# Expert stage: the third weight remainder of a block's first step goes behind the accumulation of the block before

## Chip, cores and metric

The kernel runs on one core of a Trainium2 chip. The metric is the device time of one execution in microseconds. The core has five engines with a queue of instructions each: TensorE (matmuls), VectorE, ScalarE, GpSimd and SyncE (here it only issues transfers). They are ordered against each other by semaphores. A queue is worked off in its order: an instruction that waits holds back those behind it.

## What is computed

The reference is two networks in a row on 512 tokens of 1024 features. The change lies in the last part of the first one, a mixture of 16 experts in 4 groups of 4. Each token goes to one group and in it to two experts:

```python
hid = jax.nn.silu(jnp.einsum('td,edf->tef', t, w_gate)) * jnp.einsum('td,edf->tef', t, w_up)
hid = hid * combine[..., None].astype(hid.dtype)
y = jnp.einsum('tef,efd->td', hid, w_down)
```

An expert has 256 hidden features, so its gate and up weights are 1024 x 512 together and its down weights 256 x 1024.

## The kernel before

**Blocks and steps.** Tokens are sorted by their group and cut into four blocks of 128 rows. Since a group's tokens may straddle blocks, seven passes (`STAIRS`; called blocks here, number i) cover all pairs of a row block and a group that can occur, and each pass has four steps, one for each expert of its group. So there are 28 steps, x = 0 to 27, and i = x // 4. Which row block and which group a pass has is read from tables at run time.

**Slabs.** A step needs three slabs of weights of 128 x 2048 numbers (1 MB): two for gate and up (`gate_slab(x, 0)`, `gate_slab(x, 1)`), one for down (`down_slab(x)`). They are numbered q in the order of use. Matmuls are done in three products, on a rounded part and a remainder of each operand. So each slab passes through four hands:

- SyncE loads it into one of six buffers (line 2054). The load of slab q waits until the remainder of slab q - 6 is done (`moe_lo`).
- ScalarE writes the rounded part into one of four buffers (`moe_split`, line 2543), once the slab that had the buffer, q - 4, has been used (`moe_used`).
- VectorE subtracts and writes the remainder (`moe_rest`, line 2924), which counts up `moe_lo`.
- TensorE waits for `moe_lo` and uses both.

**A step on TensorE** (loop at line 2308): the first half of gate and up of x (12 matmuls of 512 columns, lines 2266 to 2268), the transposition of the hidden values of x - 1 (line 2278), the second half of gate and up of x (12), and the down product of x - 1 (`down`, lines 2293 to 2295, 12 matmuls). The down products of a block's four steps add up in two PSUM banks. The one of the next block's first step, e == 0, overwrites them, and waits before that for `moe_acc`:

```python
                if e == 0 and i:
                    pe.wait_ge(moe_acc, i)
                pe.wait_ge(moe_hT_lo, x + 1)
```

**A step on VectorE** (loop at line 2973), in the order of its queue: the remainder of the transposed hidden values of x - 1 (`hidT_lo`, line 2976; it waits for ScalarE's rounded copy, line 2564); where x % 4 == 1 and i > 0, the accumulation of block i - 1 (`add_pair`, lines 2963 to 2971): it reads an address from a table into a register (line 2967) and adds the two banks to the sum in SBUF, then raises `moe_acc`; the remainder of the slab four behind the step's first one; the product of the gate, the up half and the routing weight (line 2997), which waits for ScalarE's Silu (line 2585) and is what TensorE transposes; and two more remainders, of the slab four behind the step's second one and four behind `down_slab(x - 1)`.

So at x = 4, whose numbers are used below, the three remainders are of the slabs 15, 16 and 17, and at x = 5 of 18, 19 and 20. Slab 17 is the first gate and up slab of x = 6, 18 the second, 19 the down slab of x = 5, 20 the first slab of x = 7.

The order on each engine is written out by hand; nothing is placed by a planner. GpSimd has no instruction inside the loop.

Of the kernel before, what the change touches and what calls it, by code (L numbers as in the profile page):

```python
# [42 lines left out]
GROUPS, PER_GROUP = 4, 4  # L43
STAIRS = TB + GROUPS - 1
EXPERT_STEPS = STAIRS * PER_GROUP
MOE_SLABS = 3 * EXPERT_STEPS
MOE_RAW, MOE_W = 6, 4
# [49 lines left out]
def gate_slab(x, part):  # L97

    return x * 3 - 1 + part if x else part


def down_slab(x):

    return 3 * x + 4 if x < EXPERT_STEPS - 1 else MOE_SLABS - 1
# [44 lines left out]
def build(nc, t):  # L149
    with ExitStack() as whole:  # L150
# [53 lines left out]
        def v1(name, i=0, rows=slice(0, P)):  # L204
            return vec[rows, V1[name].start + i:V1[name].start + i + 1]
# [2624 lines left out]
        def _(dve):  # L2830
# [91 lines left out]
            def moe_rest(q):  # L2922
                dve.wait_ge(moe_hi, q + 1)
                dve.tensor_tensor(moe_w_lo[q % MOE_W], moe_raw[q % MOE_RAW], moe_w_hi[q % MOE_W].bitcast(F32),
                                  ALU.subtract).then_inc(moe_lo, 1)
# [37 lines left out]
            def add_pair(i):  # L2963
                dve.wait_ge(moe_used, down_slab(PER_GROUP * i + PER_GROUP - 1) + 1)
                if i:
                    dve.wait_ge(moe_acc, i)
                at = dve.value_load(acc_at[0:1, i:i + 1], min_val=0, max_val=D * (TB - 1))
                for n in range(2):
                    to = acc[:, bass.ds(at + n * TOK, TOK)]
                    ins = dve.tensor_tensor(to, pd[2 + n][:], to, ALU.add)  # L2970
                ins.then_inc(moe_acc, 1)

            for x in range(EXPERT_STEPS + 1):
                if x:
                    dve.wait_ge(moe_hT_hi, x)
                    dve.tensor_tensor(hidT_lo[(x - 1) % 2], px[(x - 1) % 2][:, 0:256],
                                      hidT_hi[(x - 1) % 2].bitcast(F32), ALU.subtract).then_inc(moe_hT_lo, 1)
                if x == EXPERT_STEPS:
                    break
                i = x // PER_GROUP  # L2980
                if x % PER_GROUP == 1 and i:
                    add_pair(i - 1)
                if 1 <= x < EXPERT_STEPS - 1:
                    moe_rest(gate_slab(x, 0) + MOE_W)
                elif x == 0:
                    moe_rest(MOE_W)
                if x == EXPERT_STEPS - 1:
                    for b in range(TB - 1):
                        dve.wait_ge(y_blk_hi, b + 1)
                        dve.tensor_tensor(acc_lo[:, b * D:(b + 1) * D], acc[:, b * D:(b + 1) * D],  # L2990
                                          acc_hi[:, b * D:(b + 1) * D].bitcast(F32), ALU.subtract).then_inc(y_blk_lo, 1)
                if x % PER_GROUP == 0:
                    if i:
                        w_at = dve.value_load(weight_at[0:1, i:i + 1], min_val=0, max_val=W_COLS * TB - 5)
                w = weight[:, x:x + 1] if i == 0 else weight[:, bass.ds(w_at + x % PER_GROUP, 1)]
                dve.wait_ge(moe_silu, x + 1)
                dve.scalar_tensor_tensor(gated[x % 2], gated[x % 2], w, pd[x % 2][:, 256:512], ALU.mult,
                                         ALU.mult).then_inc(moe_hid, 1)
                if x < EXPERT_STEPS - 1:
                    moe_rest(gate_slab(x, 1) + MOE_W)  # L3000
                else:
                    for b in range(TB):
                        ins = dve.tensor_scalar(back[:, b], pos_row, v1("slot", b), None, ALU.is_equal)
                    ins.then_inc(back_ready, 1)
                if 1 <= x < EXPERT_STEPS - 1:
                    moe_rest(down_slab(x - 1) + MOE_W)
            add_pair(STAIRS - 1)
            dve.wait_ge(y_blk_hi, TB)
# [426 lines left out]
```

## Time and profile before

| what | value |
|---|---|
| median of 3 runs | 2624.4 us |
| the runs | 2622.12, 2624.4, 2628.64 us |
| profiled execution | 2626.12 us, its span 2624.3 us |
| TensorE busy | 2577.8 us, 98% of the span |
| VectorE busy | 1546.3 us, 59% |
| ScalarE busy | 1088.5 us, 41% |
| GpSimd busy | 875.4 us, 33% |

The profile is one execution. Its rows name an engine (PE is TensorE's matmuls, PEld its weight loads, DVE VectorE, ACT ScalarE, POOL GpSimd, SP SyncE; a q behind the name is the engine's sequencer), a line of the kernel, the operation and its output and inputs. Times are us from the start of the span. A matmul's row is longer than the distance to the next one, since they are pipelined; the distance of starts is what one costs. The same is so on VectorE and ScalarE, by some 0.1 us.

The expert loop lies between about 420 and 660 us of the span.

### The profile page before, as it was taken

Reading aid. Unit: us, or ns where it says so; the run is one execution under the profiler, and the core shown is the slowest. Engines: PE = TensorE matmul, PEld = TensorE weight load, DVE = VectorE, ACT = ScalarE, POOL = GpSimd, SP = SyncE. Lnnn points to the kernel's source line nnn. Section 1 sums busy time; section 2 is a strip of 40 time slices with the busy share of each in tenths; the row PEclk is TensorE's granted clock in tenths of the full one; section 3 lists DMA queues with packets and bytes.
Section 4 is the critical chain, followed back from the end, with each engine's and each line's share of the span. In section 5 each row is a group of like instructions: output and inputs, shape, how many; then the busy total and the mean of one; then the engine's idle time right before and its main releaser. Section 6 shows DMA issues by size and latency. Waiting matters only on the chain.

```text
span 2624.3 us, 32509 instructions
## 1 busy us (share of the span) xinstructions
PE 2577.8 (98%) x12950; PEld 2124.6 (81%) x12950; DVE 1546.3 (59%) x1716; ACT 1088.5 (41%) x1299; POOL 875.4 (33%) x203
## 2 busy tenths in 40 slices
PE   7999999999999999999999999999999999999998
PEld 5777788888788888888888888888888888888887
DVE  5584637999765483364765437854654464835445
ACT  6333627887425532334432223435433343422222
POOL 0211020000242443445344443433443454344444
PEclk9999988999999999999999999999999999999999
DMA  4240036998221662232333333322652232333332
GB/s 155 105 154 2 1 129 263 368 362 327 77 96 55 222 253 81 96 116 101 113 121 121 120 120 112 109 81 100 245 196 87 96 120 96 113 128 121 120 120 105
DMA packets 61292, 361.13 MB, mean 138 GB/s; under 512 B 7280, under 2 KB 8176, under 8 KB 26096
## 3 DMA queue, kind: packets, MB, share of 16 engines
q1 hardware_dynamic: 58720, 353.49, 37.6%
q10 hardware_dynamic: 2448, 5.90, 0.7%
q8 instruction: 88, 1.44, 0.2%
q14 instruction: 36, 0.29, 0.0%
HBM read 357.25 MB, written 2.10 MB: 137 GB/s over the span
## 4 chain that ended last, share of the span: by engine, by line
PE 81%; DVE 3%; ACT 1%; issue 1%; POOL 1%; DMA 0%; ACTq 0%; DVEq 0%; SPq 0%; POOLq 0%
PE pd L278 20%; PE pd L280 19%; PE pd L279 19%; PE pd L304 2%; PE pd L303 2%; PE pd L302 2%; PE pd L2268 2%; PE pd L2267 2%; PE pd L2266 2%; DVE sb_y_lo L1967 1%; PE pd L2293 1%; PE pd L2295 1%; PE pd L2294 1%; PE pd L2223 1%; PE px L2424 1%
## 5 line engine op out<-in xcount | busy, mean ns | idle before, releaser
L228 POOL TENSOR_TENSOR sb_w_lo<-sb_raw,sb_w_hi 128x2048 fp32r<-128x2048 f32 x175 | 819.3, 4682 | 1596.8 <-ACT sb_w_hi L219 1596.8
L278 PE MATMUL pd<-sb_h_hi,sb_w_hi 128*128 128x512 f32 x1600 | 631.7, 395 | 3.0 <-DVE sb_h_lo L580 2.4
L279 PE MATMUL pd<-sb_h_lo,sb_w_hi 128*128 128x512 f32 x1600 | 624.0, 390 | 0.0
L280 PE MATMUL pd<-sb_h_hi,sb_w_lo 128*128 128x512 f32 x1600 | 623.9, 390 | 0.0
L219 ACT CAST sb_w_hi<-sb_raw 128x2048 fp32r<-128x2048 f32 x181 | 346.1, 1913 | 410.1 <-PE pd L280 311.2
L278 PE MATMUL pd<-sb_y_hi,sb_w_hi 128*128 128x512 f32 x944 | 369.1, 391 | 1.2 <-DVE sb_y_lo L1967 0.8
L280 PE MATMUL pd<-sb_y_hi,sb_w_lo 128*128 128x512 f32 x944 | 367.4, 389 | 0.0
L279 PE MATMUL pd<-sb_y_lo,sb_w_hi 128*128 128x512 f32 x944 | 367.4, 389 | 0.0
L278 PEld LDWEIGHTS pd<-sb_h_hi,sb_w_hi 128*128 128x128 f32 x1600 | 301.0, 188 | 68.6 <-issue 5.2
L280 PEld LDWEIGHTS pd<-sb_h_hi,sb_w_lo 128*128 128x128 f32 x1600 | 301.0, 188 | 63.2
L279 PEld LDWEIGHTS pd<-sb_h_lo,sb_w_hi 128*128 128x128 f32 x1600 | 301.2, 188 | 61.4 <-issue 0.5
L278 PEld LDWEIGHTS pd<-sb_y_hi,sb_w_hi 128*128 128x128 f32 x944 | 177.2, 188 | 41.5 <-DVE sb_y_lo L1967 4.6
L1967 DVE TENSOR_TENSOR sb_y_lo<-sb_T,sb_y_hi 128x512 fp32r<-128x512 f32 x80 | 187.9, 2388 | 35.8 <-ACT sb_y_hi L1941 28.5
L280 PEld LDWEIGHTS pd<-sb_y_hi,sb_w_lo 128*128 128x128 f32 x944 | 177.2, 188 | 37.1
L279 PEld LDWEIGHTS pd<-sb_y_lo,sb_w_hi 128*128 128x128 f32 x944 | 177.2, 188 | 36.4
L2009 DVE SCALAR_TENSOR_TENSOR sb_xT<-pd,sb_lay,sb_xT 128x512 f32<-128x512 f32 x80 | 56.8, 747 | 155.8 <-PE pd L280 152.1
L1936 ACT ACTIVATE sb_T<-pd 128x512 f32<-128x512 f32 x60 | 32.6, 595 | 203.9 <-PE pd L280 203.9
L594 DVE CUSTOM_DVE_ANT_0 sb_QK<-sb_QK,sb_Y 128x1024 f32<-128x1024 f32 x32 | 77.2, 2448 | 67.8 <-ACT sb_Y L2710 44.9
L302 PE MATMUL pd<-sb_w_hi,sb_h_hi 128*128 128x512 f32 x288 | 112.6, 391 | 0.0
L304 PE MATMUL pd<-sb_w_lo,sb_h_hi 128*128 128x512 f32 x288 | 112.1, 389 | 0.0
L303 PE MATMUL pd<-sb_w_hi,sb_h_lo 128*128 128x512 f32 x288 | 112.1, 389 | 0.0
L3241 DVE TENSOR_TENSOR sb_T<-sb_T 128x512 f32<-128x512 f32 x64 | 45.0, 744 | 105.6 <-ACT sb_T L1936 103.6
(591 smaller groups left out, 3740.1 us busy)
## 6 DMA issues: line engine op xcount, KB each, us to landing
sb_raw<-in_slabs SPq DMA_DIRECT2D x190, 1024.0 KB, 4.8
sb_moe_raw<-in_moe SPq DMA_DIRECT2D x56, 1024.0 KB, 6.6
sb_raw<-in_moe SPq DMA_DIRECT2D x28, 1024.0 KB, 6.2
sb_QK<-in_ada SPq DMA_DIRECT2D x32, 512.0 KB, 5.4
sb_V<-in_ada SPq DMA_DIRECT2D x32, 512.0 KB, 5.5
sb_M<-in_ada SPq DMA_DIRECT2D x16, 512.0 KB, 3.9
sb_Y<-in_ada SPq DMA_DIRECT2D x16, 512.0 KB, 5.8
sb_MG<-in_ada SPq DMA_DIRECT2D x16, 512.0 KB, 5.9
```

The costliest lines, as they stand in the source:

```text
L219: act.copy(w_hi[j][:], raw[j][:]).then_inc(w_hi_ready[j], 1)
L228: pool.tensor_tensor(w_lo[j][:], raw[j][:], w_hi[j][:].bitcast(F32), ALU.subtract).then_inc(w_lo_ready[j], 1)
L278: pe.matmul(out, w_hi[j][:, cols], hi[:, k], start=(k == 0), stop=False)
L279: pe.matmul(out, w_hi[j][:, cols], lo[:, k], start=False, stop=False)
L280: last = pe.matmul(out, w_lo[j][:, cols], hi[:, k], start=False, stop=(k == KT - 1))
L302: pe.matmul(pd[b][:], hi[:, k, toks], w_hi[j][:, cols], start=(k == 0), stop=False)
L303: pe.matmul(pd[b][:], lo[:, k, toks], w_hi[j][:, cols], start=False, stop=False)
L304: last = pe.matmul(pd[b][:], hi[:, k, toks], w_lo[j][:, cols], start=False, stop=(k == KT - 1))
L594: dve.tensor_tensor_reduce(tiles[slot], tiles[slot], row, 1.0, 0.0, ALU.mult, ALU.add, into).then_inc(ada_used, 1)
L1967: dve.tensor_tensor(y_lo[:, bass.ds(2 * n + f, 1)], T[:, tj + f:tj + f + 1], y_hi[:, bass.ds(2 * n + f, 1)].bitcast(F32), ALU.subtract).th ...
L2009: ins = dve.scalar_tensor_tensor(to, bank, lay[:, bass.ds(gate + tile + 2 * j + f, 1)], to, ALU.mult, ALU.add)
L2266: pe.matmul(pd[x % 2][:], hi[:, k], moe_w_hi[s][:, cols], start=(k == 0), stop=False)
```

## The change

On VectorE, the remainder of slab `down_slab(x - 1) + 4` is no longer computed at the end of a step with x % 4 == 0, the first step of a block. It is computed in the step behind it, directly behind the accumulation (`add_pair`) of the block before and ahead of that step's first remainder. The slab is the one four behind the down slab of the last step of the block before. This happens in the steps 4, 8, 12, 16, 20 and 24; at x = 0 there is no such remainder. The order of the remainders among themselves stays (15, 16, 17, 18, ...), and so do all counts on the semaphores.

```diff
@@ -2980,6 +2980,7 @@
                 i = x // PER_GROUP
                 if x % PER_GROUP == 1 and i:
                     add_pair(i - 1)
+                    moe_rest(down_slab(x - 2) + MOE_W)
                 if 1 <= x < EXPERT_STEPS - 1:
                     moe_rest(gate_slab(x, 0) + MOE_W)
                 elif x == 0:
@@ -3002,7 +3003,7 @@
                     for b in range(TB):
                         ins = dve.tensor_scalar(back[:, b], pos_row, v1("slot", b), None, ALU.is_equal)
                     ins.then_inc(back_ready, 1)
-                if 1 <= x < EXPERT_STEPS - 1:
+                if 1 <= x < EXPERT_STEPS - 1 and x % PER_GROUP:
                     moe_rest(down_slab(x - 1) + MOE_W)
             add_pair(STAIRS - 1)
             dve.wait_ge(y_blk_hi, TB)
```

## Rows read from the trace of the kernel before

**Rows 1.** The page, busy time of each engine, share of the span, instructions.
```profile
PE 2577.8 (98%) x12950; PEld 2124.6 (81%) x12950; DVE 1546.3 (59%) x1716; ACT 1088.5 (41%) x1299; POOL 875.4 (33%) x203
```

**Rows 2.** Table of stretches (busy us, count; clock, DMA share, GB/s), x = 5 and 6.
```profile
core 0: us, PE busy (x) PEld busy (x) DVE busy (x) ACT busy (x) POOL busy (x), PEclk, DMA share, GB/s
461.30:470.30 9.00, 8.73 (x40) 6.86 (x39) 8.98 (x8) 6.38 (x5) 0.00 (x0) 1.00 0.98 366
470.30:478.70 8.40, 8.40 (x39) 6.93 (x38) 7.36 (x6) 7.33 (x6) 0.00 (x0) 1.00 0.96 363
```

**Rows 3.** Waits in the expert stage: total us, times, longest; TensorE and its weight loads.
```profile
PEld pd L2293 <- issue: 4.0, 6, 0.7
...
PE pd L2293 <- issue: 1.6, 6, 0.3
```

**Rows 4.** Timeline of TensorE: start, duration, instruction [idle before]; first and sixth gap.
```profile
466.80 0.39 PE L2268 MATMUL pd<-sb_moe_w_lo,sb_sorted_blk 128*128 128x512 f32 x1
467.45 0.47 PE L2293 MATMUL pd<-sb_w_hi,sb_hidT_hi 128*128 128x512 f32 x1 [0.27 <-issue]
...
470.30 0.39 PE L2266 MATMUL pd<-sb_w_hi,sb_sorted_blk 128*128 128x512 f32 x1
...
638.51 0.47 PE L2293 MATMUL pd<-sb_w_hi,sb_hidT_hi 128*128 128x512 f32 x1 [0.28 <-issue]
```

**Rows 5.** Timeline of VectorE from the end of x = 4 to x = 7.
```profile
463.53 2.29 DVE L2924 TENSOR_TENSOR sb_w_lo<-sb_moe_raw,sb_w_hi 128x2048 fp32r<-128x2048 f32 x1
465.74 0.41 DVE L2976 TENSOR_TENSOR sb_hidT_lo<-px,sb_hidT_hi 128x256 fp32r<-128x256 f32 x1
466.08 1.28 DVE L2970 TENSOR_TENSOR sb_MG<-pd,sb_MG 128x512 f32 x2
467.27 2.28 DVE L2924 TENSOR_TENSOR sb_moe_w_lo<-sb_raw,sb_moe_w_hi 128x2048 fp32r<-128x2048 f32 x1
469.47 0.47 DVE L2997 SCALAR_TENSOR_TENSOR sb_T<-sb_T,sb_lay,pd 128x256 f32<-128x256 f32 x1
469.86 2.28 DVE L2924 TENSOR_TENSOR sb_moe_w_lo<-sb_raw,sb_moe_w_hi 128x2048 fp32r<-128x2048 f32 x1
472.50 2.29 DVE L2924 TENSOR_TENSOR sb_w_lo<-sb_moe_raw,sb_w_hi 128x2048 fp32r<-128x2048 f32 x1 [0.35 <-ACT sb_w_hi L2543]
474.71 0.42 DVE L2976 TENSOR_TENSOR sb_hidT_lo<-px,sb_hidT_hi 128x256 fp32r<-128x256 f32 x1
...
483.12 0.42 DVE L2976 TENSOR_TENSOR sb_hidT_lo<-px,sb_hidT_hi 128x256 fp32r<-128x256 f32 x1
```

**Rows 6.** Timeline of ScalarE: copy of hidden values, x = 5, and cast of slab 20.
```profile
464.48 0.37 ACT L2564 CAST sb_hidT_hi<-px 128x256 fp32r<-128x256 f32 x1 [0.98 <-PE px L2278]
...
470.55 1.92 ACT L2543 CAST sb_w_hi<-sb_moe_raw 128x2048 fp32r<-128x2048 f32 x1 [1.05 <-PE pd L2295]
```

**Rows 7.** Line 2967, register load, first and last of seven; line 2970, the adds.
```profile
L2967 DVEq TENSOR_LOAD <-sb_small x7: 303/311/327, 464.9 to 665.9; - x7
...
L2970 DVE TENSOR_TENSOR sb_MG<-pd,sb_MG x14: 678/680/692, 466.1 to 667.2; 128x512 f32 x14
```

**Rows 8.** Timeline at the stage's end: last matmul of the last down product, accumulation.
```profile
665.42 0.39 PE L2295 MATMUL pd<-sb_moe_w_lo,sb_hidT_hi 128*128 128x512 f32 x1
...
666.58 1.29 DVE L2970 TENSOR_TENSOR sb_MG<-pd,sb_MG 128x512 f32 x2 [6.28 <-PE pd L2295]
```

**Rows 9.** Timeline of TensorE, x = 6: transposition, down product of step 5, next step.
```profile
473.02 0.38 PE L2278 MATMUL px<-sb_ident,sb_T 128*128 128x128 f32 x2
...
475.99 0.39 PE L2293 MATMUL pd<-sb_moe_w_hi,sb_hidT_hi 128*128 128x512 f32 x1
...
478.71 0.39 PE L2266 MATMUL pd<-sb_w_hi,sb_sorted_blk 128*128 128x512 f32 x1
```

**Rows 10.** Load of slab 23, time to landing (455 to 490 us), cast of slab 23.
```profile
466.01 0.34 SPq L2054 DMA_DIRECT2D sb_moe_raw<-in_moe  x1
...
DMA to landing us min/median/max: 4.8/5.2/6.3
...
478.96 1.92 ACT L2543 CAST sb_moe_w_hi<-sb_moe_raw 128x2048 fp32r<-128x2048 f32 x1 [0.50 <-PE pd L2295]
```

## Prediction

> **What bounds the kernel now.** I read the page first: TensorE is busy for 98% of the span [rows 1], so nothing the change does on VectorE counts unless it opens or closes a gap on TensorE. The stretch that the change touches is the expert stage, where seven blocks of four steps follow each other. The table by step of the second block [rows 2] shows one step of about 8.4 us, and the step in which the accumulation falls is 9.0 us long, with VectorE busy for 8.98 of them against 7.36 in the next. So VectorE is full there and nearly full elsewhere. The list of waits [rows 3] has six gaps of TensorE before the down product (line 2293), 1.6 us together on the matmuls and 4.0 us on their weight loads. They are put down to "issue", but the wait that stands there in the code is the one for `moe_acc`, and the accumulation is what ends just before: the second of its two adds ends at 467.36 and the matmul starts at 467.45 [rows 4, 5]. That is 0.09 us from release to start, which I use below for VectorE to TensorE.
>
> The gap's whole price is read from TensorE's own rows [rows 4]. The last gate/up matmul starts at 466.80. One pitch is 0.227 us (12 matmuls in 2.72 us, 475.99 to 478.71 [rows 9]), so the down product could start at 467.03. It starts at 467.45 and takes until 470.30, 2.85 us instead of 2.72, because the matmuls come a little slower after a stop. The price is 470.30 minus (467.03 + 2.72) = **0.55 us a block**. The same gap stands before the down product of each of six blocks; the last is at 638.51 [rows 4]. All there is to win is 6 x 0.55 = 3.3 us.
>
> **What the change removes and adds.** No instruction is added or dropped. In each block but the first, one 2.21 us remainder (slab 17 in the block that I follow; start to start on VectorE, 463.53 to 465.74 [rows 5]) moves from before `hidT_lo` and the two adds to behind them. SP's ring counts remainders, so one load per block is issued later, too. I write the new order of VectorE out from these rows, in the trace's own times, with x = 5 as the step of the accumulation.
>
> 1. Behind slab 16's remainder VectorE is free at 463.53 at the latest. It now goes straight to `hidT_lo` of step 4, which needs ScalarE's copy: 464.48 + 0.37 = 464.85 [rows 6]. It starts at about 464.88 instead of 465.74, 0.86 us earlier. VectorE stands still for 1.35 us meanwhile, and this is the cost that nothing gives back.
>
> 2. The adds need a register load (line 2967), which the trace shows at 464.9, right after that copy, though VectorE is still in a remainder [rows 5, 7]. It was hidden; now it is partly bare. The case where the load is bare stands at the end of the stage: load 665.9, first add 666.58 [rows 7, 8], 0.68 us. So the first add starts at 464.9 + 0.7 = 465.60, where `hidT_lo` alone would let it start at 464.88 + 0.34 = 465.22 (0.34 from [rows 5]). Bounds: hidden after all, 465.22; begun only when `hidT_lo` is through (465.30), and then the 0.77 us from the last matmul's end, 665.42 + 0.39, to 666.58 [rows 8], 466.07. I take 465.60, because the load was at 464.9 while the engine was busy, so it does not wait for the engine.
>
> 3. The adds end at 465.60 + 1.28 = 466.88 instead of 467.36 [rows 5]. With 0.09 us that is 466.97, before 467.03. **TensorE's gap closes**: down(4) runs from 467.03 to 469.75, and TensorE is 0.55 us ahead.
>
> 4. Then come four remainders and one product until `hidT_lo` of step 5, where there were three and one. By the pitches of [rows 5] (adds 1.19, remainder 2.21, product 0.39): slab 17 at 466.79, slab 18 at 469.00, product at 471.21, slab 19 at 471.60, slab 20 at 473.81, `hidT_lo` of step 5 at **476.02** instead of 474.71. Of the 0.35 us for which VectorE waited for ScalarE before slab 20, nothing is left.
>
> 5. TensorE's needs, shifted by 0.55 us [rows 9]: slab 17 at 469.75 (ready 469.08), slab 18 at 472.61 (471.29), the product for the transpose at 472.47 (471.68), slab 19 at 475.44 (473.89). All met; the tightest has 0.67 us. ScalarE's cast of slab 20 began at 470.55, behind down(4); half a microsecond earlier now, it is no bound [rows 6]. But down(5) also needs `hidT_lo` of step 5, and could start at 475.99 - 0.55 = 475.44. It gets it at 476.02 + 0.42 + 0.09 = **476.53**. This is a new gap of 1.09 us, one step behind the old one.
>
> 6. After that stop down(5) takes 2.85 us again, as down(4) did [rows 4], and ends at 479.38; before it ended at 478.71 [rows 9]. **Net +0.67 us a block.** TensorE's gain in step 5 doesn't enter: the new start hangs on VectorE's chain, which is anchored at the copy of 464.85.
>
> 7. Is it carried on? VectorE goes on at 476.36: slab 21, product, slab 22 until 481.17. Slab 23's cast began at 478.96, 0.25 us behind the end of down(5) [rows 9, 10], so now at 479.63 and until 481.55; the remainder runs to 483.78, and `hidT_lo` of step 6 is there at 484.20 (before 483.12 + 0.42 [rows 5]). Down(6) needs it at 479.38 + 2.72 + 2.97 = 485.07 [rows 9]. From there VectorE waits for ScalarE again, as before. The lateness ends within two steps, and each block pays once.
>
> 8. SP: the load behind slab 17's remainder went out at 466.01; now at about 469.2. Landing took at most 6.3 us [rows 10], so it is there by 475.5, and ScalarE wants it at 478.96. The next ones are 1.2 to 2 us later and have more room. Cost nothing; GpSimd has no work in this stage [rows 2].
>
> Sum: 6 x 0.67 = **+4.0 us**. The profiled execution took 2626.12 us (span 2624.30); it would take 2630.1. The median of the runs, 2624.4, is 1.7 us below the profiled one, and I carry the difference: **2628.4 us**. With the bounds of step 2 the new start moves by -0.38 or +0.47 us: +0.29 a block (1.7 us, 2626.1) to +1.14 a block (6.8 us, 2631.2).
>
> On the register load a page of the Trainium skill can be weighed against the rows: "DMA: Bandwidth & Descriptors", section "Latency and other measured facts", gives a floor of about 600 ns for a `tensor_load`. The trace shows 0.68 us from the load's start to the add at the place where nothing hides it [rows 7, 8]. An estimate by the page would put the adds 0.08 us earlier and the sum at 3.5 instead of 4.0 us.
>
> **Rivals.**
> *The gap goes and nothing replaces it.* This is faster: 6 x 0.55 = 3.3 us, 2621.1 us. It holds if VectorE's chain from 464.88 is 1.1 us shorter than by my pitches. For it: VectorE is busy for only 7.36 us of the step behind [rows 2], so it seems to have a microsecond to spare. Against: that microsecond lies behind step 5's four remainders, and even with the load wholly hidden the chain ends 0.7 us too late. 10 in 100.
> *The load waits for the engine, or a second place is hit.* The upper bound of step 2, +6.8 us, 2631.2 us; slower still only if the slab margin of 0.67 us in step 5 goes as well. At 466.07 for the adds slab 17 would be ready at 469.55, still before 469.75. To reach 0.3% each block would have to lose 1.3 us. 10 in 100.
> *It does nothing.* If VectorE's copy dependence were late enough that the order didn't matter, both gaps would stay as they are, 2624.4 us. The adds' start is set by the remainder in front of them (463.53 + 2.21 = 465.74 [rows 5]), not by the copy at 464.85, so this is unlikely: 5 in 100.
> *The forecast*, a new gap before the down product one step later: 75 in 100.
>
> **How the numbers follow.** About 0.3%, 7.9 us, is what a measurement of this kernel can tell from no change. Neither the whole gain (3.3 us) nor the upper bound (6.8 us) reaches it, so within 0.3% gets 0.94; slower by more needs something beyond the bound, 0.04; faster by more 0.02. The range takes in the bounds 2626.1 and 2631.2, and the scatter of the runs shown (2622.12 to 2628.64 around 2624.4, so 2 to 4 us) on both sides, and most of the gap-only case: 2621.5 to 2633.
>
> **What would show it.** Right: in the trace after, the six gaps before line 2293 sit one down product later; `hidT_lo` starts about 0.9 us sooner in the accumulation's step and 1.3 us later in the next; four remainders stand without a break between the adds and it; a block takes 34.9 us instead of 34.2 (first and sixth gap at 467.45 and 638.51 [rows 4], 171.06 / 5 = 34.21). Step 2 is wrong if the first add does not start 0.7 us behind the copy. The prediction fails if the down product of step 5 starts without a gap (then 2621), or if TensorE also waits for slab 17 or 18 (then above 2631).

## The result, and the profile after

| | before | changed |
|---|---|---|
| median of 20 runs each | 2625.63 us | 2631.20 us |
| ratio | | 1.0023, 95% interval 1.0016 to 1.0030 |
| span of the profiled execution | 2624.3 us | 2629.5 us |
| first to last transposition of the expert stage (line 2278) | 228.2 us | 232.8 us |

The changed kernel is slower by 4 to 8 us (0.23% of 2626 is 6.0 us; the medians are 5.6 us apart). The forecast was 2628.4 us, 4.0 us more than before, and the measured median is 2631.2.

The last row of the table is the measure that I use for all kernels below. It comes from the rows that give the first and the last start of one line, rounded to 0.1 us, so a length can be off by 0.1 us. Before and after:

```profile
L2278 PE MATMUL px<-sb_ident,sb_T x56: 270/271/328, 430.4 to 658.6; 128*128 128x128 f32 x56
```
```profile
L2278 PE MATMUL px<-sb_ident,sb_T x56: 270/271/327, 430.2 to 663.0; 128*128 128x128 f32 x56
```

So 4.6 us are lost between the first and the last of these. The waits of the changed kernel in the stage (total, times, longest) show where, and answer to [rows 3]:

```profile
DVE sb_hidT_lo L2976 <- ACT sb_hidT_hi L2564: 8.3, 6, 1.4
PEld pd L2293 <- DVE sb_w_lo L2924: 7.7, 6, 1.3
...
PE pd L2293 <- DVE sb_hidT_lo L2976: 5.3, 6, 0.9
DVE sb_MG L2970 <- issue: 2.2, 6, 0.4
PEld pd L2293 <- issue: 1.6, 6, 0.3
```

TensorE's idle time before the down product was 1.6 us in six gaps and is 5.3 us in six gaps, and it is now put down to `hidT_lo`. Two waits of VectorE are new: 6 x 1.4 us for ScalarE's copy of the hidden values, and 2.2 us on the register load. (The weight loads' wait is put down to a remainder, `w_lo`. The one that ends just before is slab 20's, at 475.92, and the down product doesn't need it; it needs slab 19's, which ended at 473.72. What ends last is `hidT_lo`, at 476.26, as the matmul's row says.)

TensorE's timeline, which answers to [rows 4, 9]. Everything in this execution lies some 0.17 us (0.13 to 0.18) earlier than in the one before, up to the first accumulation:

```profile
466.62 0.39 PE L2268 MATMUL pd<-sb_moe_w_lo,sb_sorted_blk 128*128 128x512 f32 x1
466.85 0.45 PE L2293 MATMUL pd<-sb_w_hi,sb_hidT_hi 128*128 128x512 f32 x1
...
469.68 0.39 PE L2266 MATMUL pd<-sb_w_hi,sb_sorted_blk 128*128 128x512 f32 x1
...
475.14 0.39 PE L2268 MATMUL pd<-sb_moe_w_lo,sb_sorted_blk 128*128 128x512 f32 x1
476.41 0.47 PE L2293 MATMUL pd<-sb_moe_w_hi,sb_hidT_hi 128*128 128x512 f32 x1 [0.88 <-DVE sb_hidT_lo L2976]
...
479.25 0.39 PE L2266 MATMUL pd<-sb_w_hi,sb_sorted_blk 128*128 128x512 f32 x1
...
511.39 0.47 PE L2293 MATMUL pd<-sb_moe_w_hi,sb_hidT_hi 128*128 128x512 f32 x1 [0.88 <-DVE sb_hidT_lo L2976]
...
651.32 0.47 PE L2293 MATMUL pd<-sb_moe_w_hi,sb_hidT_hi 128*128 128x512 f32 x1 [0.88 <-DVE sb_hidT_lo L2976]
```

The old gap is gone as idle time: line 2293 starts one pitch, 0.23 us, behind the last gate/up matmul. A short stop is left, though. The twelve matmuls of this down product take 2.83 us (466.85 to 469.68) instead of 2.72, and the step takes 8.52 us from transposition to transposition, in the later blocks 8.57 to 8.59, instead of 8.41. The adds still end only just in time. One down product later there is the new one: 476.41 instead of 475.14 + 0.23 = 475.37, 1.04 us late. A block takes (651.32 - 476.41) / 5 = 34.98 us, before 34.21.

VectorE's timeline answers to [rows 5]:

```profile
461.04 2.29 DVE L2924 TENSOR_TENSOR sb_w_lo<-sb_moe_raw,sb_w_hi 128x2048 fp32r<-128x2048 f32 x1 [0.25 <-ACT sb_w_hi L2543]
464.70 0.42 DVE L2976 TENSOR_TENSOR sb_hidT_lo<-px,sb_hidT_hi 128x256 fp32r<-128x256 f32 x1 [1.37 <-ACT sb_hidT_hi L2564]
465.44 1.29 DVE L2970 TENSOR_TENSOR sb_MG<-pd,sb_MG 128x512 f32 x2 [0.32 <-issue]
466.65 2.28 DVE L2924 TENSOR_TENSOR sb_w_lo<-sb_moe_raw,sb_w_hi 128x2048 fp32r<-128x2048 f32 x1
468.85 2.28 DVE L2924 TENSOR_TENSOR sb_moe_w_lo<-sb_raw,sb_moe_w_hi 128x2048 fp32r<-128x2048 f32 x1
471.05 0.47 DVE L2998 SCALAR_TENSOR_TENSOR sb_T<-sb_T,sb_lay,pd 128x256 f32<-128x256 f32 x1
471.44 2.28 DVE L2924 TENSOR_TENSOR sb_moe_w_lo<-sb_raw,sb_moe_w_hi 128x2048 fp32r<-128x2048 f32 x1
473.64 2.28 DVE L2924 TENSOR_TENSOR sb_w_lo<-sb_moe_raw,sb_w_hi 128x2048 fp32r<-128x2048 f32 x1
475.85 0.41 DVE L2976 TENSOR_TENSOR sb_hidT_lo<-px,sb_hidT_hi 128x256 fp32r<-128x256 f32 x1
```

The reader sees the price (1.37 us idle ahead of the first row's successor), the bare register load (0.32 us), and then an unbroken chain of adds, remainder, remainder, product, remainder, remainder up to `hidT_lo` at 475.85.

### The profile page after: what moved, and what is told of

Read it like the earlier page. It is cut to its first block, busy times and chain, and to the rows that moved or that the text cites. A ratio compares the mean times of both kernels' runs of the same rounds, so it can differ in the third digit from the quotient of the medians.

```text
span 2629.5 us, 32509 instructions
## 1 busy us (share of the span) xinstructions
PE 2579.4 (98%) x12950; PEld 2125.0 (81%) x12950; DVE 1544.9 (59%) x1716; ACT 1088.6 (41%) x1299; POOL 875.4 (33%) x203
## 4 chain that ended last, share of the span: by engine, by line
PE 79%; DVE 5%; issue 1%; ACT 1%; POOL 1%; DMA 0%; DVEq 0%; ACTq 0%; SPq 0%; POOLq 0%
PE pd L278 20%; PE pd L280 19%; PE pd L279 19%; PE pd L303 2%; PE pd L302 2%; PE pd L304 2%; PE pd L2268 1%; PE pd L2266 1%; PE pd L2267 1%; DVE sb_y_lo L1967 1%; DVE sb_moe_w_lo L2924 1%; PE pd L2293 1%; PE pd L2295 1%; PE pd L2294 1%; DVE sb_w_lo L2924 1%
```

## The experiments

All eight were run with their times against the kernel before. "Stage" is the distance from the first to the last start of line 2278, read as above.

| kernel | stage, us | to before (228.2) | ratio of times, 95% interval |
|---|---|---|---|
| e1 load ahead of the wait | 229.9 | +1.7 | 1.0003, 0.9994 to 1.0012 |
| e2 next step's remainder deferred too | 226.8 | -1.4 | 0.9996, 0.9986 to 1.0005 |
| e3 old order, `moe_acc` by halves | 225.1 | -3.1 | 0.9985, 0.9976 to 0.9994 |
| e4 changed order, `moe_acc` by halves | 232.7 | +4.5 | 1.0015, 1.0006 to 1.0025 |
| e5 remainder ahead of the adds | 236.2 | +8.0 | 1.0019, 1.0010 to 1.0029 |
| e6 e2 with e1 and halves | 225.4 | -2.8 | 0.9989, 0.9977 to 1.0001 |
| e7 e3 again | 224.9 | -3.3 | 0.9987, 0.9975 to 0.9999 |
| e8 changed kernel again | 232.7 | +4.5 | 1.0017, 1.0006 to 1.0027 |

**e1: is the register load on the chain?** Against the changed kernel:

```diff
+                if x % PER_GROUP == 1 and x // PER_GROUP:
+                    at = acc_address(x // PER_GROUP - 1)
                 if x:
                     dve.wait_ge(moe_hT_hi, x)
...
-                    add_pair(i - 1)
+                    add_pair(i - 1, at)
```

> The changed kernel, with the register load of the accumulation's address (line 2967) issued before VectorE waits for ScalarE's copy of the hidden values, so that it lies beside a remainder. My theory: the start of the down product of the block's first step hangs on VectorE's chain copy, hidT_lo, load, adds, four remainders, product, hidT_lo; the bare part of the load is in it. In the profile of the changed kernel the first add starts 0.74 us behind hidT_lo (464.70 to 465.44), where one pitch of hidT_lo is 0.34. So the first add starts 0.34 us behind it, the gap of TensorE before the down product (0.88 us idle) shrinks by 0.40 us in each of six blocks, a block takes 34.58 us instead of 34.98, and the kernel takes 2.4 us less than the changed kernel, about 2.2 us more than before in the expert stage (ratio to before about 1.001). Rival: the load is not on that chain (the engine would not have been free, or TensorE waits for a slab's remainder). Then the six gaps stay 0.88 us and the ratio stays 1.002.

The add follows `hidT_lo` at once, and the gap of TensorE shrinks (VectorE, then TensorE):

```profile
468.78 0.42 DVE L2980 TENSOR_TENSOR sb_hidT_lo<-px,sb_hidT_hi 128x256 fp32r<-128x256 f32 x1 [1.37 <-ACT sb_hidT_hi L2564]
469.12 1.28 DVE L2972 TENSOR_TENSOR sb_MG<-pd,sb_MG 128x512 f32 x2
```
```profile
480.07 0.47 PE L2293 MATMUL pd<-sb_moe_w_hi,sb_hidT_hi 128*128 128x512 f32 x1 [0.57 <-DVE sb_hidT_lo L2980]
...
514.56 0.47 PE L2293 MATMUL pd<-sb_moe_w_hi,sb_hidT_hi 128*128 128x512 f32 x1 [0.57 <-DVE sb_hidT_lo L2980]
```

A block takes 34.49 us, 0.49 less than in the changed kernel, more than the 0.40 expected. The gap itself shrinks by less, from 0.88 us idle to 0.57 and not to 0.48, because TensorE arrives at it sooner: the short stop at the accumulation is gone too (all steps but the gap's take 8.41 us, where the changed kernel has one of 8.57 to 8.59 in each block). The expectation took the bare load from the first block, where the add comes 0.74 us behind `hidT_lo`. From the second on it is 0.80 (499.62 to 500.42), and 0.80 - 0.34 = 0.46. The rival (load not on the chain) falls. A loss of 1.7 us against the kernel before is still there: with the load hidden, VectorE is still too late.

**e2: is it the fourth remainder that makes `hidT_lo` late?** Against the changed kernel:

```diff
                     add_pair(i - 1)
+                if x >= PER_GROUP and x % PER_GROUP in (1, 2):
                     moe_rest(down_slab(x - 2) + MOE_W)
...
-                if 1 <= x < EXPERT_STEPS - 1 and x % PER_GROUP:
+                if 1 <= x < EXPERT_STEPS - 1 and not (x >= PER_GROUP and x % PER_GROUP in (0, 1)):
```

> The changed kernel, in which the third remainder of the next step too (x % 4 == 1, slab 20 in the block of x = 4) goes behind hidT_lo of the step after it. My theory: hidT_lo of that step was late by 1.04 us because four remainders stood in front of it; with three it is done at about 474.1 in the times of the changed kernel, where TensorE wants it at 475.4. Both gaps are gone, six times 0.55 us less than before: 3.3 us faster than before (ratio 0.9987) and about 8 us faster than the changed kernel. Slab 20 is ready at 476.3, wanted at 478.1. The tightest place is one step on: hidT_lo of step 6 is done at about 483.6, wanted at 483.8, so a gap of up to 0.1 us may appear there (2.7 us faster instead of 3.3). Rival: VectorE has no slack in these steps and the lateness only moves on: then a gap of some 0.5 to 1 us a block stands before the down product of step 6, and the kernel is as slow as the changed one.

Both gaps are gone, as my theory says, and the kernel is faster than the changed one; from the kernel before its times can't be told apart (0.9986 to 1.0005). The stage is 1.4 us shorter than before, not 2.7 to 3.3. The waits name the difference:

```profile
PE px L2278 <- DVE sb_T L2999: 0.7, 1, 0.7
PEld pd L2293 <- issue: 2.7, 12, 0.3
```

There are twelve short stops, two a block, where the release comes just as TensorE could start. They show no idle time on the matmuls, yet steps take 8.52 us (460.11 to 468.63, first transposition to first) and 8.49 instead of 8.41, in later blocks up to 8.59 and 8.49, together 1.3 us in six blocks. And 0.7 us are lost once at the end of the stage (the last distance of transpositions is 6.63 us, before 5.95), where VectorE arrives later for the last product. I had expected at most 0.1 us for the tight place and nothing for the other. 3.3 - 1.3 - 0.7 = 1.3, and 1.4 was measured.

Even this gain doesn't last in the execution that was profiled. Right behind the last transposition the matmuls come every 0.43 us instead of 0.23, seven times in a row (two of these distances, and one behind them):

```profile
655.23 0.63 PE L2304 MATMUL px<-sb_y_hi,sb_h_lo 128*128 128x512 f32 x1
655.66 0.63 PE L2304 MATMUL px<-sb_y_hi,sb_h_hi 128*128 128x512 f32 x1
656.09 0.63 PE L2304 MATMUL px<-sb_y_hi,sb_h_lo 128*128 128x512 f32 x1
...
658.71 0.39 PE L2304 MATMUL px<-sb_y_hi,sb_h_hi 128*128 128x512 f32 x1
658.94 0.39 PE L2304 MATMUL px<-sb_y_hi,sb_h_lo 128*128 128x512 f32 x1
```

The clock granted to TensorE is 0.50 there (655 to 658 us), the lower of its two levels; in the profiles before, of e3 and of e6 it is 1.00 at this place. Ahead of it TensorE had been idle for 0.70 and 1.24 us in quick succession. That costs 1.6 us: from the first transposition to the first matmul of line 278, behind the stage, it is 248.2 us (674.59 - 426.36), before 248.0. The length of the stage doesn't contain it. Whether the other executions of e2 have it too, and whether the longer stop brings it on, no run shows.

**e3 and e7: what is the old gap worth by itself?** Against the kernel before:

```diff
-                    ins = dve.tensor_tensor(to, pd[2 + n][:], to, ALU.add)
-                ins.then_inc(moe_acc, 1)
+                    dve.tensor_tensor(to, pd[2 + n][:], to, ALU.add).then_inc(moe_acc, 1)
...
                 if e == 0 and i:
-                    pe.wait_ge(moe_acc, i)
+                    pe.wait_ge(moe_acc, 2 * i - 1)
...
                     for n in range(2):
+                        if e == 0 and i and kt == 0 and n == 1:
+                            pe.wait_ge(moe_acc, 2 * i)
```

> The kernel before, in its old order, with moe_acc raised by each of the two adds; TensorE waits for the first add before the first bank of the down product and for the second before the second bank. This measures the price of the old gap by itself. The first add ends at 466.76, TensorE could start at 467.03; the second ends at 467.36 and is wanted at 467.71. So the gap closes without a remainder being moved: six times 0.55 us, 3.3 us faster than before (ratio 0.9987), a block takes 33.66 us instead of 34.21. Rival: the gap is the cost of the wait itself or of TensorE's queue (the profile put it down to issue): then it stays at 0.27 us idle and the ratio is 1.000.

> The kernel before with moe_acc raised by each add, again, on the same chip as the changed kernel. From the first time: no gap, 225.1 us from the first to the last transposition of the expert stage against 228.2 before, so 3.1 us faster, ratio 0.9985 to 0.999. If the first result came from another cause than the gap (a low granted clock elsewhere in the compared runs), it does not repeat.

No gap stands before the down product in either profile, and the stage is 3.1 and 3.3 us shorter. So 0.55 us a block was the right price for a gap whose row shows 0.27 us idle (0.42 us of late start and 0.13 us of slower matmuls behind it), and the gap was the wait for the second add, though the profile called it "issue". e3's stage is, with e7's, the shortest here, and both ratios lie below 1 with their whole interval. Its stage in the first profile:

```profile
L2278 PE MATMUL px<-sb_ident,sb_T x56: 270/271/332, 426.3 to 651.4; 128*128 128x128 f32 x56
```

**e4: does the changed kernel still wait for the accumulation?** The edit of e3, made to the changed kernel.

> The changed kernel with the same two-step moe_acc as in the run before. My theory: the old gap is closed in the changed kernel already, and the new one hangs on VectorE's chain, which this does not touch. So six gaps of 0.88 us idle before the down product of the block's first step but one stay, a block takes 34.98 us, ratio to before about 1.002. Rival: part of the loss is TensorE still waiting for the accumulation in the changed kernel. Then this one is faster than the changed kernel by that part.

It does, but that costs nothing. Without this wait the accumulation's step takes 8.41 us instead of 8.52 to 8.59, so the short stop there goes. Yet releasing the accumulation earlier brings nothing; the new gap is the same loss as seen from a TensorE that is ready 0.11 to 0.17 us sooner:

```profile
PE pd L2295 <- DVE sb_hidT_lo L2977: 6.2, 6, 1.1
```

The first gap moved from 0.88 to 0.99 us idle, later ones to 1.05, just what the stop had cost, and a block still takes 34.98 us (480.24 to 515.22). I had written that they stay 0.88; the block time is as expected. That is the plainest proof that the new start hangs on VectorE's chain and not on where TensorE stands.

**e5: does VectorE's standing still cost by itself?** Against the changed kernel:

```diff
                 if x % PER_GROUP == 1 and i:
-                    add_pair(i - 1)
                     moe_rest(down_slab(x - 2) + MOE_W)
+                    add_pair(i - 1)
```

> The changed kernel with the moved remainder one place earlier: behind hidT_lo, but ahead of the accumulation. It makes the old gap larger and leaves everything behind the adds with the work it had in the kernel before. My theory: TensorE pays for a late accumulation one for one. In the times of the kernel before: hidT_lo at 464.88, remainder 465.22, adds 467.43 (the register load is hidden beside the remainder) to 468.71, so the down product starts at about 468.80 where it could at 467.03, and ends at 471.65 instead of 470.30. Six gaps of about 1.6 us idle before the down product of the fourth step of a block, none one step on (hidT_lo of step 5 is done at 476.5, wanted at 477.3); a block takes 35.56 us, six times 1.35 = 8.1 us more than before, ratio 1.003. Rival: VectorE's standing still for 1.4 us before hidT_lo is what costs, wherever the remainder goes. Then the gap one step on is there again and the block takes 34.9 to 35.0 us as in the changed kernel.

VectorE stands still for the same 1.37 us here, yet the gap one step on is not there. The late accumulation is, as expected:

```profile
469.71 0.47 PE L2293 MATMUL pd<-sb_w_hi,sb_hidT_hi 128*128 128x512 f32 x1 [1.62 <-issue]
...
505.26 0.47 PE L2293 MATMUL pd<-sb_w_hi,sb_hidT_hi 128*128 128x512 f32 x1 [1.61 <-issue]
```

A block takes 35.55 us (expected 35.56) and the stage is 8.0 us longer (expected 8.1). The rival falls as it was stated, a block of 34.9 to 35.0 us with the gap one step on. That standing still is free isn't shown: `hidT_lo` of step 5 comes at 476.96, which is 11.18 us behind that of step 4 (465.78), and in the changed kernel it is 11.15 (464.70 to 475.85). It is as late as there. No gap shows because TensorE is late itself and wants it only for 478.24.

The ratio, 1.0019, is below the expected 1.003, which lies just outside its interval (1.0010 to 1.0029). The granted clocks account for most of this. At equal mean granted clock of the execution e5 is slower by what its stage says, or a little more: at 0.994 its mean is 2631.5 us against 2623.1 before, at 0.992 it is 2635.4 against 2626.3. All twelve of its runs had one of these two clocks, but eleven of the 35 runs before had 0.990 or 0.991, and their means are 2631.9 and 2629.1 us.

**e6: were e2's short stops the register load and the late second add?** e2 with the edits of e1 and e3.

> The kernel of the second experiment (both third remainders behind hidT_lo of the next step), with the register load ahead of the wait for ScalarE's copy, and moe_acc raised by each add. In the second experiment TensorE made two short stops a block, at 463.08 and 480.01, where the adds and hidT_lo of step 6 came 0.1 us too late; steps took 8.52 and 8.49 us instead of 8.41. My theory: with VectorE's chain 0.4 us shorter both stops go, every step takes 8.41 to 8.42 us, the expert stage from the first to the last transposition is about 1.2 us shorter than in the second experiment (225.6 us against 226.8), and the ratio to before is about 0.9990. Rival: the short stops are the price of VectorE's order itself (the remainders lie too close to TensorE's need) and stay.

The stops are gone. Transpositions follow each other every 8.41 us through the blocks, and the stage is 225.4 us (expected 225.6):

```profile
473.49 0.38 PE L2278 MATMUL px<-sb_ident,sb_T 128*128 128x128 f32 x2
481.90 0.38 PE L2278 MATMUL px<-sb_ident,sb_T 128*128 128x128 f32 x2
490.31 0.38 PE L2278 MATMUL px<-sb_ident,sb_T 128*128 128x128 f32 x2
```

Of e2's 0.7 us idle at the stage's end 0.5 stay (the last distance is 6.33 us, before 5.95), so e6 is no better than e3, which needs no reordering at all.

**e8: the changed kernel again.**

> The changed kernel as it is, again. The expert stage took 4.6 us more than before (232.8 us from the first to the last transposition against 228.2); the runs gave 5.6 us between the medians. My theory: the change is worth the 4.6 us only, and the rest is where the granted clock fell in each execution; ratio 1.0018, interval down to 1.001. Rival: something outside the expert stage costs a microsecond too; then the difference stays at 6 us or more.

The stage is 232.7 us long again, and the ratio is 1.0017, that is 4.5 us. The interval, 1.6 to 7.1 us, doesn't exclude the rival's 6 us by itself; the profiles speak against it, see below.

## Why the prediction was right

**The bound.** TensorE's gaps set the time, and VectorE was full in the accumulation's step: shown by [rows 2, 3] and by every kernel above, whose stage lengths follow from TensorE's stops.

**Steps 1 and 2, the start of the adds.** Forecast: `hidT_lo` 0.86 us sooner, the first add 0.72 us behind it. Taking off the 0.17 us by which this execution is ahead, `hidT_lo` came at 464.87 (forecast 464.88) and the add at 465.61 (465.60). From the start of `hidT_lo` to the add it is 0.74 us, in later blocks 0.80. The page of the Trainium skill on DMA ("DMA: Bandwidth & Descriptors", "Latency and other measured facts") gives a floor of some 600 ns for such a load; the estimate by it was 465.52 for the add, 0.09 us too early. The trace doesn't contradict it as a floor: from the load's start (464.7) to the add (465.44) it is 0.7 us. e1 shows that this load is 0.46 us of the chain.

**Step 3, the old gap closes:** right for the idle time. That the down product then takes 2.72 us was wrong: with 0.06 us of margin it took 2.83, and the accumulation's step kept 0.11 to 0.18 us of stop a block. It doesn't enter the sum, because the next start hangs on VectorE (e4). The gap's whole worth, 3.3 us, was measured by e3 and e7: 3.1 and 3.3.

**Steps 4 and 5, the chain.** Forecast: `hidT_lo` of step 5 at 476.02; measured 475.85 + 0.17 = 476.02. No slab was late. The new gap was forecast as 1.09 us and is 1.04.

**Step 6, net per block.** Forecast 0.67 us; measured 34.98 - 34.21 = 0.77, in the first block 0.71 (479.25 + 0.17 against 478.71). This is the term that was too small, by a seventh. Two parts show in rows. From the end of `hidT_lo` to the matmul it is 0.15 us (475.85 + 0.41 to 476.41), where I had taken 0.09 from the old gap. And the bare load is 0.06 us longer from the second block on. Six times 0.1 is the 0.6 us between 4.0 forecast and 4.6 measured in the stage.

**Step 7, recovery within two steps:** right. `hidT_lo` of step 6 started at 483.66 and the next down product at 484.94 without a gap.

**Step 8, the loads.** Right that they cost nothing, wrong in a detail. The load of slab 23 went out at 469.11 (forecast 469.2), but landings took up to 8.2 us, not 6.3:

```profile
DMA to landing us min/median/max: 4.7/6.9/8.2
```

Its cast started at 479.50, behind the down product, 2 us and more after the latest landing.

**The rivals.** "The gap goes and nothing replaces it" was the result of e3, by another edit. It failed for the change for the reason given: the microsecond of slack lies behind four remainders. "The load waits for the engine" has 2631.2 us as its time, which is just the measured median, but that is chance: its mechanism would put the adds at 466.07 and cost 6.8 us, and the add came at 465.61 and the stage lost 4.6. "A second place is hit" did not happen. "It does nothing" fell.

**The rest of the time.** The median is 2.8 us above the forecast. 1.2 us of that is the base, 2624.4 us from three runs and 2625.6 from twenty. The other 1.6 us is the difference of the medians, 5.6 us where 4.0 were forecast; 0.6 of it is step 6.

Between the two profiled executions 5.2 us differ, and the stage explains 4.6, less the 0.17 us head start. Up to the first matmul behind the stage the changed kernel is 4.43 us later (682.78 against 678.35), and it stays so up to 2001 us (line 2424's last start 2001.3 against 1996.9). The remaining 0.8 us come at the end, where the clock granted to TensorE was lower in the changed kernel's profile. There the last matmuls of line 358 start every 0.21 us instead of every 0.11. In the four microseconds from 12 to 8 before the end, before and after:

```profile
2612.30:2616.30 4.00, 3.05 (x25) 2.69 (x24) 0.57 (x3) 1.74 (x3) 0.97 (x1) 0.91 0.00 0
```
```profile
2617.50:2621.50 4.00, 3.07 (x17) 2.69 (x17) 0.53 (x2) 1.11 (x2) 1.79 (x1) 0.68 0.00 0
```

(The last three numbers are the granted clock, the DMA share and GB/s.) This end differs between executions of equal code too. From the last start of line 350 to the end of the span it is 10.5 us before and 11.3 in the changed kernel, but also 11.3 in e3 and 10.4 in e7, which are the same code. So it isn't a price of the change.

The ratio of the times allows for 4.2 to 7.9 us, and e8's for 1.6 to 7.1. The stage's 4.6 us lie in both; the forecast's 4.0 us lie just below the first. Whether a further microsecond, as the first ratio's middle would have it, belongs to the change isn't settled by the times. The profiles show none: from the last transposition of the stage to the last start of line 2424 it is 1338.3 us in both.

## What to carry to other kernels

A gap is closed only if the engine that was late has the time; moving its work behind the wait moves the lateness to the next consumer, and the first thing to write out is its queue from the moved instruction to that consumer. Moving work from before a wait to behind it also loses the time for which the engine now waits (here 1.37 us, for a start that was 0.42 us late). Where an accumulation is made of several instructions, releasing the consumer after the first of them (e3) can close the gap without any reordering.

## What the runs showed of the hardware

**A stop costs more than its idle time.** A gap with 0.27 us idle in its row cost TensorE 0.55 us a block (e3, e7): the matmul started 0.42 us behind its pitch, since the row before it is longer than a pitch, and the twelve behind took 0.13 us more. Stops without any idle time in the matmuls' rows cost 0.05 to 0.18 us each (e2: steps of 8.46 to 8.59 us instead of 8.41; the changed kernel: 8.52 to 8.59 at the accumulation, 8.41 without the wait in e4).

**The register load was hidden only beside earlier work.** Its rows are 0.30 to 0.33 us for the load, 0.19 and 0.02 us for what follows. Behind a wait it delayed the add by 0.40 to 0.46 us beyond the pitch of `hidT_lo`; ahead of the wait it delayed nothing (e1).

**Executions of equal code reach the stage at different times.** The kernels are the same up to the expert stage, but the first transposition came at 426.2 us in e8 and at 434.0 in e4. It goes with the mean granted clock of the stretch before it, 0.99 in e8 and 0.96 in e4 (the third number from the right), and in all ten profiles the order is the same: 0.99 goes with 426.2 to 426.4 us, 0.98 with 430.2 and 430.4, 0.97 with 430.5 and 431.3, 0.96 with 434.0 and 434.3.

```profile
20.00:390.00 370.00, 353.95 (x2865) 280.29 (x2865) 215.32 (x429) 162.38 (x324) 58.71 (x15) 0.99 0.22 76
```
```profile
20.00:390.00 370.00, 354.60 (x2825) 280.67 (x2824) 211.42 (x422) 161.45 (x323) 58.69 (x15) 0.96 0.22 74
```

These 8 us are more than the whole effect of any kernel here but e5. For changes of this size the length of the stage is the better measure, as long as the rows behind it are read too (in e2 a lower clock just behind the stage took back its 1.4 us). It repeated within 0.2 us (232.8 and 232.7 for the changed kernel, 225.1 and 224.9 for e3 and e7), where the intervals of the ratios, from 11 to 20 runs, leave some 2 to 3 us either way.
